# A streaming encoder layer with 32 experts: 16 KB weight rows in 2 MB pieces, and the prompt's output projection inside the sample's attention

## The reference

```python
z = rms(x) @ w_in                          # 1024 x 3080
fox:  8 heads x 64, causal, softmax(q k / 8 + c_q - c_k) v      # c: cumulative log forget
diff: 4 heads, (softmax(q1 k1) - lam * softmax(q2 k2)) v, chunk mask, then rms over 128
h = x + concat(fox, diff) @ w_out
logits = rms(h) @ w_router + b             # 32 experts, top 4, softmax over the 4
y = h + sum over the 4 of gate * (act(rms(h) @ w_gate_up[e] + b) @ w_down[e] + b)
act = min(glu, 7) * sigmoid(1.702 glu) * (clip(lin, -7, 7) + 1)
```

## Time and profile before

| | |
|---|---|
| median of 3 runs | 1375.59 us (1375.3 to 1377.74) |
| profiled execution | 1374.94 us, span 1373.0 us |
| TensorE (PE) busy | 1286.1 us, 94% |
| VectorE (DVE), ScalarE (ACT), GpSimd (POOL) busy | 368.3, 207.2, 145.0 us |
| first pair of experts starts | 418.93 us |
| moved by DMA | 447.1 MB, mean 326 GB/s |

### The profile page before, as it was taken

How to read it: one execution, slowest core, us unless ns; L and a number is a source line. 1 busy time by engine, 2 the same in 40 slices (tenths; PEclk the granted TensorE clock), 3 DMA queues, 4 the chain that set the end, 5 groups by cost and what they waited for, 6 DMA issues and landing times.

```text
span 1373.0 us, 16981 instructions
## 1 busy us (share of the span) xinstructions
PE 1286.1 (94%) x6083; PEld 564.9 (41%) x6084; DVE 368.3 (27%) x959; ACT 207.2 (15%) x524; POOL 145.0 (11%) x340
## 2 busy tenths in 40 slices
PE   6799999999989999999999999999899999999987
PEld 3344445555454443434434344343434434343422
DVE  4223233557251321212212131121213112121311
ACT  5011322255140110101101010010101001010100
POOL 0022300000002101101011010101101010110000
PEclk9999955589989999999999999999999999999997
DMA  8801540046536999999999999999999999999994
GB/s 286 314 32 69 186 152 1 1 153 212 189 136 261 422 413 420 417 416 420 414 422 414 420 416 417 419 414 422 416 419 417 417 420 414 422 413 420 416 417 175
DMA packets 98284, 447.10 MB, mean 326 GB/s; under 512 B 13729, under 2 KB 14002, under 8 KB 65474
## 3 DMA queue, kind: packets, MB, share of 16 engines
q1 hardware_dynamic: 98242, 446.55, 80.8%
HBM read 441.66 MB, written 4.86 MB: 325 GB/s over the span
## 4 chain that ended last, share of the span: by engine, by line
PE 58%; DMA 19%; SPq 17%; DVE 2%; issue 2%; POOL 1%; ACT 1%; DVEq 0%; POOLq 0%; ACTq 0%
DMA arena<-in_w_gate_up 18%; PE psum L1536 15%; SPq L496 13%; PE psum L1568 10%; PE psum L1519 6%; PE psum L1285 5%; PE psum L1433 3%; PE psum L1581 3%; PE psum L1389 3%; PE psum L1341 2%; SPq L386 2%; PE psum L1369 1%; PE psum L1321 1%; PE psum L1557 1%; PE psum L1400 1%
## 5 line engine op out<-in xcount | busy, mean ns | idle before, releaser
L1536 PE MATMUL psum<-arena 128*64 128x512 f32 x2048 | 449.4, 594 | 26.9 <-DMA arena<-in_w_gate_up 26.4
L1536 PEld LDWEIGHTS psum<-arena 128*64 128x64 f32 x2048 | 151.0, 137 | 323.3 <-issue 323.3
L1568 PE MATMUL psum<-arena 128*64 128x512 f32 x1024 | 225.4, 598 | 0.0
L1193 DVE TENSOR_SCALAR arena<-psum 128x256 f32<-128x256 f32 x64 | 27.0, 422 | 439.4 <-PE psum L1536 437.5
L1568 PEld LDWEIGHTS psum<-arena 128*64 128x64 f32 x1024 | 72.5, 138 | 151.7 <-issue 151.7
L1285 PE MATMUL psum<-arena 128*128 128x512 f32 x288 | 127.8, 600 | 0.0
L826 ACT ACTIVATE arena<-arena 128x256 f32<-128x256 f32 x64 | 26.7, 417 | 595.1 <-DVE arena L1193 595.1
L1581 PE MATMUL psum<-arena 128*128 128x512 f32 x192 | 92.5, 616 | 13.1 <-ACT arena L834 13.1
L1519 PEld LDWEIGHTS psum<-arena 128*128 128x128 f32 x768 | 88.5, 194 | 16.1 <-issue 16.1
L1519 PE MATMUL psum<-arena 128*128 128x128 f32 x768 | 91.5, 279 | 3.8 <-POOL arena L593 3.8
L586 POOL COPY arena<-arena 128x6 f32 (+1 forms) x16 | 3.0, 188 | 784.9 <-PE psum L1568 712.9
(11 more groups left out here) (216 smaller groups left out, 893.8 us busy)
## 6 DMA issues: line engine op xcount, KB each, us to landing
arena<-in_w_gate_up SPq DMA_DIRECT2D x256, 1024.0 KB, 22.5
arena<-in_w_down SPq DMA_DIRECT2D x128, 1024.0 KB, 18.5
arena<-in_w_in SPq DMA_DIRECT2D x6, 2048.0 KB, 19.8
arena<-in_cache_fox_k SPq DMA_DIRECT2D x8, 512.0 KB, 3.6
arena<-in_cache_diff_k SPq DMA_DIRECT2D x8, 512.0 KB, 4.4
arena<-in_cache_fox_v SPq DMA_DIRECT2D x8, 512.0 KB, 4.1
arena<-in_cache_diff_v SPq DMA_DIRECT2D x8, 512.0 KB, 5.7
arena<-in_w_out SPq DMA_DIRECT2D x4, 1024.0 KB, 7.6
```

The source lines that it names most:

```text
L1536: last = mm(banks[n][half], XT[u][:, k, half], slot(s[x])[:, 512 * n:512 * (n + 1)], start=False, stop=(k == 7), skip_group_check=True)
L1568: last = mm(banks[hf][half], actT[:, 2 * i + c, half], w, start=False, stop=(i == 3 and c == 1), skip_group_check=True)
```

## The change

- Weights: 12 pieces of 2 MB for each pair through 8 slots. Partition p now holds rows 8p to 8p + 7 of an expert's matrix, so a piece is 16 KB in one run of each partition: two rows of w_gate_up, or four of w_down. From one partition to the next the source steps 64 KB in w_gate_up and 32 KB in w_down. `piece_done` counts after every second k.
- What is multiplied has to follow that order: `scale` writes x2n with its columns regrouped, the activations' products are written with a step of 128 elements, the gains come from a second load (gcol_x) in that order. The transposes of the activations wait for all four quarters.
- The output projection of the prompt's two tiles (n = 0 to 3) is cut into eight halves, one in each of the last eight steps of the sample's attention, all in bank 7, each half in two parts around `turn_probs`. The first half of n waits for `residual(n - 1)`. All mixes now go to bank 6, and mix e waits for the copy of mix e - 1. `turn_out` moves ahead of `turn_probs`.
- The last steps are put in another order: projections 4 and 5 are split around the transposes and the logits, squares 0 and 1 come ahead of the sample's diff norm on ScalarE, routing of tile 1 ahead of the copy of tile 2 on VectorE, gate 0 behind the table. The loads of x_prompt into y are issued earlier, behind `d_done`.

```diff
-PIECES = 24
-RING = 16
-PIECE_W = 2048
-LEAD = 4
+PIECES = 12
+RING = 8
+SLOT_W = 2048
+PIECE_W = 4096
+LEAD = 2
+EARLY = 4
...
+        def out_bank(n):
+            return banks[7] if n < EARLY else banks[n]
+
+        def early_out(i):
+
+            j = i - s_unit[0] - 8
+            return (j // 2, j % 2) if 0 <= j < 2 * EARLY else None
...
-            if r < 16:
-                k = r // 2
-                return io["w_gate_up"][0, bass.ds(e, 1), k * P:(k + 1) * P, :].rearrange("a p n -> p (a n)")
-            k = 2 * ((r - 16) // 2)
-            return io["w_down"][0, bass.ds(e, 1), k * P:(k + 2) * P, :].rearrange("a (c p) n -> p (a c) n", p=P)
+            name, i = ("w_gate_up", r // 2) if r < 8 else ("w_down", (r - 8) // 2)
+            rows_ = io[name][0, bass.ds(e, 1)].rearrange("a (p q) n -> p (a q n)", p=P)
+            return rows_[:, PIECE_W * i:PIECE_W * (i + 1)]
...
+            sp.dma_start(gcol_x, io["ffn_norm"][0].rearrange("(p k) -> p k", p=P)).then_inc(s_gx, 16)
...
+                if b == 6:
+                    sp.wait_ge(scored, s_unit[0])
+                    sp.wait_ge(d_done, DIFF_H)
+                    for t in range(2):
+                        sp.dma_start(y[:, t], io["x_prompt"][0, P * t:P * (t + 1), :]).then_inc(s_xr, 16)
...
-                nc.scalar.activation(x2n[:, t], y[:, t], ACT.Copy, scale=stat[:, 24 + t:25 + t]).then_inc(h_n, 1)
+                nc.scalar.activation(x2n[:, t].rearrange("s (k p) -> s p k", k=8), y[:, t].rearrange("s (p k) -> s p k", k=8),
+                                     ACT.Copy, scale=stat[:, 24 + t:25 + t]).then_inc(h_n, 1)
...
             square(0)
+            square(1)
+            ac.wait_ge(d_ms, DIFF_H + 1)
+            nc.scalar.activation(dsq_s, dsq_s, ACT.Sqrt).then_inc(d_rt, 1)
             root(0)
+            root(1)
             hT_evac(0)
+            hT_evac(1)
             scale(0)
-            square(1)
-            root(1)
+            square(2)
+            root(2)
+            hT_evac(2)
+            scale(1)
+            scale(2)
             gates(0)
...
                     maxes(i + 2)
+                if early_out(i - 1) and early_out(i - 1)[1] == 1:
+                    residual(early_out(i - 1)[0])
                 if 0 <= i + 1 < NA:
                     norms(i + 1)
...
-            residual(2)
-            mean(0)
+            invert(0)
+            invert(1)
             hT_evac(0)
-            residual(3)
-            invert(0)
-            mean(1)
             route(0)
-            gate(0)
             residual(4)
             hT_evac(1)
-            invert(1)
             residual(5)
-            hT_evac(2)
             mean(2)
             route(1)
+            hT_evac(2)
             invert(2)
             route(2)
...
-                    nc.vector.tensor_tensor(act[:, 256 * n:256 * (n + 1)], ta[n % 2], sg[n % 2], ALU.mult
+                    nc.vector.tensor_tensor(act_rows[:, 32 * n:32 * (n + 1)],
+                                            ta[n % 2].rearrange("s (p q) -> s p q", q=8),
+                                            sg[n % 2].rearrange("s (p q) -> s p q", q=8), ALU.mult
                                             ).then_inc(act_ready, 1)
...
-                if e >= 2:
-                    pe.wait_ge(mix_copied, e - 1)
-                O, pt, g = banks[6 + e % 2], pT[e % 2], x["g"]
+                if e >= 1:
+                    pe.wait_ge(mix_copied, e)
+                O, pt, g = mixed_at(e), pT[e % 2], x["g"]
...
+                if 0 <= i - 2 < NA and att[i - 2]["where"] == "s":
+                    turn_out(i - 2)
+                if early_out(i):
+                    n, part = early_out(i)
+                    project_out(n, range(4 * part, 4 * part + 2))
                 if 0 <= i < NA and att[i]["turn"]:
                     turn_probs(i)
+                if early_out(i):
+                    project_out(n, range(4 * part + 2, 4 * part + 4))
                 if 0 <= i - 1 < NA and att[i - 1]["turn"]:
                     mix(i - 1)
-                if 0 <= i - 2 < NA and att[i - 2]["where"] == "s":
-                    turn_out(i - 2)
...
-            project_out(2)
+            pe.wait_ge(mix_copied, NT)
+            project_out(4, range(2))
             pe.wait_ge(d_sq, DIFF_H + 1)
-            pe.wait_ge(mix_copied, NT)
             mm(banks[3], C["ones"], dsq_s, start=True, stop=True).then_inc(d_sum, 1)
             turn_rows(0)
-            project_out(3)
+            project_out(4, range(2, 4))
+            project_out(5, range(4))
+            turn_rows(1)
             logits(0)
             pe.wait_ge(d_done, DIFF_H + 1)
-            project_out(4)
-            turn_rows(1)
-            project_out(5)
+            project_out(4, range(4, 8))
+            project_out(5, range(4, 8))
             logits(1)
...
                 pe.wait_ge(y_added, at_(6, Y_BASE))
+                pe.wait_ge(act_ready, at_(4, 4))
                 for c in range(8):
-                    if c % 2 == 0:
-                        pe.wait_ge(act_ready, at_(4, c // 2 + 1))
```

More of the change, by code:

```diff
@@ L121, in build @@
         gcol = at(take(20), 20)
+        gcol_x = at(take(8), 8)
         lf0 = cur
@@ L159, in build @@
         junk = at(t0, 1024)
-        xs = [at(14 * PIECE_W + 1024 * t, 1024) for t in range(4)]
-        cache = [at((12 + 2 * i) * PIECE_W, 4096).rearrange("p (s t n) -> p s t n", s=4, t=2) for i in range(2)]
+        xs = [at(14 * SLOT_W + 1024 * t, 1024) for t in range(4)]
+        cache = [at((12 + 2 * i) * SLOT_W, 4096).rearrange("p (s t n) -> p s t n", s=4, t=2) for i in range(2)]
         ffv, ffl, nc_p = at(t0 + 2560, NTOK), at(t0 + 1024, NTOK), at(nc0, NKEY_P)
@@ L486, in _ @@
                 sp.dma_start(bdn2[E * hf:E * (hf + 1)], io["b_down"][0, :, 512 * hf:512 * (hf + 1)]).then_inc(s_bdn, 16)
-            for n_ in range(12, 16):
-                sp.dma_start(slot(n_ + LEAD - RING), piece_src(0, n_)).then_inc(ring_in[n_ + LEAD - RING], 16)
+            for n_ in (6, 7):
+                sp.dma_start(piece_slot(n_ + LEAD - RING), piece_src(0, n_)).then_inc(ring_in[n_ + LEAD - RING], 16)
             def refill(it, j):
@@ L1148, in _ @@
                                          AX.X, ALU.max))
+            gate(0)
             gate(1)
@@ L1425, in cum_cached, with project_out @@
                 last.then_inc(cum_done, 1)
-            def project_out(n):
+            def project_out(n, ks):
                 t, hf = n // 2, n % 2
-                if n >= 2:
-                    pe.wait_ge(y_added, n - 1)
-                for k in range(8):
+                if n == 0 and ks[0] == 0:
+                    pe.wait_ge(s_wout, 64)
+                    pe.wait_ge(d_done, DIFF_H)
+                elif n < EARLY and ks[0] == 0:
+                    pe.wait_ge(y_added, n)
+                for k in ks:
                     wv = slot(k // 2).rearrange("p (k n) -> p k n", k=2)
-                    last = mm(banks[4 + n % 2], oT[:, k, P * t:P * (t + 1)], wv[:, k % 2, 512 * hf:512 * hf + 512],
+                    last = mm(out_bank(n), oT[:, k, P * t:P * (t + 1)], wv[:, k % 2, 512 * hf:512 * hf + 512],
                               start=(k == 0), stop=(k == 7))
-                last.then_inc(o_done, 1)
+                if ks[-1] == 7:
+                    last.then_inc(o_done, 1)
             for i in range(-3, NA + 2):
@@ L1531, in pair @@
                 for k in range(8):
-                    s = [arrived(2 * k + x) for x in range(2)]
+                    if k % 2 == 0:
+                        s = [arrived(k + x) for x in range(2)]
                     for n in range(4):
@@ L1535, in pair @@
                             half = slice(SLOTS * x, SLOTS * (x + 1))
-                            last = mm(banks[n][half], XT[u][:, k, half], slot(s[x])[:, 512 * n:512 * (n + 1)],
+                            c0 = 2 * FF * (k % 2) + 512 * n
+                            last = mm(banks[n][half], XT[u][:, k, half], piece_slot(s[x])[:, c0:c0 + 512],
                                       start=False, stop=(k == 7), skip_group_check=True)
-                            if n == 3:
+                            if n == 3 and k % 2 == 1:
                                 last.then_inc(piece_done, 1)
@@ L1566, in pair @@
                                 half = slice(SLOTS * x, SLOTS * (x + 1))
-                                w = slot(s[x])[:, D * c + 512 * hf:D * c + 512 * (hf + 1)]
-                                last = mm(banks[hf][half], actT[:, 2 * i + c, half], w, start=False,
-                                          stop=(i == 3 and c == 1), skip_group_check=True)
-                                if c == 1 and hf == 1:
+                                w = piece_slot(s[x])[:, D * c + 512 * hf:D * c + 512 * (hf + 1)]
+                                last = mm(banks[hf][half], actT[:, 4 * i + c, half], w, start=False,
+                                          stop=(i == 1 and c == 3), skip_group_check=True)
```

(1 more changed line is left out.)

97 lines of the change are left out of this document (46 added, 51 removed).

## The result

| | before | after |
|---|---|---|
| median, us | 1375.28 (1370.98 to 1377.74, 6 runs) | 1381.44 (1379.82 to 1383.89, 6 runs) |
| ratio | | 1.0049, 95% interval 1.0032 to 1.0066 |
| profiled execution, span | 1373.0 | 1379.8 |
| first pair's gate-up starts | 418.93 | 440.40 |
| its last gate-up matmul ends (last pair) | 1334.1 | 1339.9 |

The account below looks back on a forecast made before the run. The prediction took the experts' weight stream as the bound, with the front adding one for one. Stage -16.4, front +17.7 and last pair +0.5 gave +1.8 on 1374.94: about 1376.5 us, own range 1371 to 1382.

Parts of the forecast that it names:

- Rate: Experts' weight stream: 16 KB runs reach 430 GB/s instead of 423 and 410, a gain of 23.3 us.
- Rival 3: Weight stream gains nothing over 8 KB runs: 423 GB/s, 1390 us, chance 0.14; or 387 GB/s, 1473 us, 0.03.
- 2 MB pieces give 3.5 us back at both ends: Experts' stream starts 3.5 us later, and two k instead of one follow the last piece, 3.5 us more.
- Strided products cost nothing: Activation products on VectorE, written with a step of 512 bytes, stay at 0.43 us each.
- Rival 4: Strided products make VectorE the bound of a pair, from 1.1 us each; at 1.74 us each, 1423 us; chance 0.05.
- Last pair +0.5: In the last expert pair, which has no gather, the transposes' wait for all four products shows: +0.5 us.
- Mixes +6.8: Six steps of the sample's attention: with one bank, mixes wait for the copy of the turned output, +6.8 us.
- Adding +3.9: First halves of projections 1, 2, 3 wait for the previous one's residual on VectorE: 1.3 us three times.
- Tile 1's transposes +2.5: Behind attention, tile 1's transposes wait for tile 0's copies, with too little TensorE work to cover: +2.5 us.
- Clock +1.7: Small work ahead of 6.9 us of projection after attention lowers TensorE's clock: 0 to 3.4 us, half taken.
- Rival 1: The front's waits shrink where VectorE or ScalarE gain by the same delay: half the cost, 1367.5 us; chance 0.20.
- Rival 5: Clock falls in the sample's attention's six steps with new waits, doubling 4.3 us of TensorE each: +26, 1402 us; 0.07.

Follow-up runs that it names:

- the run with the old layout: Front and contiguous products of the kernel before, with 2 MB pieces made of whole row blocks (8 and 4 KB runs): 1382.24 us, ratio 1.0057 against before.
- the weight part alone: Kernel before with only the 2 MB pieces, their layout, strided scale and products, and the second gain load: 1360.91 us, ratio 0.9906 against before.
- the front alone: Kernel before, its weights kept, with only the moved projections, one bank for mixes and new order behind attention: 1392.81 us, ratio 1.0124 against before.

## Why the prediction was right, and where not

The forecast was 1376.5 with a range of its own from 1371 to 1382; 1381.4 is at its upper end. Its structure holds: two parts that add, one of -16 on the stream, one of +18 in the front. The two profiles are 6.8 us apart where +1.8 was forecast; of the 5 us between, 4 lie in the front, and the clock is the term that was too small. (The sum on record, 1374.94 + 1.8, is 1376.7, and 1377.4 from the median; it was written as 1376.5.)

- **Rate.** 430 forecast, 428.5 measured. The line through the earlier trace rows was right, its slight overshoot costs 2.5 us over the stream. Rival 3 (423 or less) is out, and the run with the old layout shows that the size of a piece is not the cause.
- **2 MB pieces give 3.5 us back at both ends.** 7.25 - 3.8 = 3.4 at the start, 7.09 - 3.65 = 3.4 at the end. Stage -15.7, forecast -16.4. A pair 58.73, forecast 58.6.
- **Strided products cost nothing.** Wrong in size, right in effect. They take 0.61 us instead of 0.43, hidden in 15 pairs. Rival 4 decides from 1.1 us, so its price was off and its place right. The Trainium skill's rule on new 16-byte lines (SBUF — State Buffer, Door 1) is borne out as to its sign: 0.43 to 0.61 us on VectorE, 1.15 to 2.05 us for the scale on ScalarE, 192 to 335 ns for a weight load. It gives no size, so rival 4 did not follow from it. As the prediction itself says, no row had a write with such a step; that all other rows agree was no evidence.
- **Last pair +0.5.** It was +2.15. The run with 2 MB pieces and contiguous products has 7.56 us there for the 6.84 of before, so waiting for all four products costs 0.7; the step 0.44 (4.48 against 4.04 of wait); the rest, 1.0, is the clock, which was down when the transposes came. The down product was 1.15 shorter, again by the clock; in the weight part alone it took 16.09 us, as before the change.
- **Mixes +6.8.** The six steps grew by 8.5 us, some 6.5 by waits and 2 by clock; undoing it brought the first pair 8.1 us forward. The first four steps grew by 0.95, 0.4, 1.05 and 1.2, as read.
- **Adding +3.9.** Forecast as three times 1.3. The waits were 1.13, 1.14 and 0.27; undoing the first two gave 2.8. In the last steps nothing stands ahead of the turned output, and TensorE already waits there for the copy of the mix. That is 0.42 us three times that I did not name, and it takes the place of the gaps which I let the projections fill (-1.2).
- **End of attention +1.6.** The last mixes stand bare, with gaps of 0.68, 0.41 and 0.32 us, where 0.91 was.
- **Tile 1's transposes +2.5, tile 2's copies +2.0.** 1.99 in this profile, 1.12 in four others with the same order; and 2.95 - 1.27 = 1.7.
- **The gain's load +0.4.** It can't be seen: from kernel to kernel the sample's attention began anywhere between 292.8 and 295.9 us.
- **Clock +1.7.** This is the term that failed. The projection of 6.9 us took 9.02 (+2.1), tile 0's logits 3.32 for 1.87 (+1.4), the first gather 8.32 for 7.17 (+1.2), the attention +2: 6.7 in all. I had split the clock in two, a term for one place and a rival of 26 us for another. What happened lies between: with the new waits the clock fell in the sample's attention in three profiles of three, without them in none of nine, and each such place cost 1 to 3.5 us. Not all of it is due to waits: the first gather took 8.05 us with the front of before too, in the run with the old layout. The mean clock of whole runs says the same: 0.940 to 0.942 in the change, 0.947 to 0.951 before.
- **Sum of the front** 17.7 forecast, 21.5 in the profile (22.6 counted from the start of the six steps, which came 1.2 us earlier by chance), 17 by the ratio of the front alone.

Rival 1 (half the front's cost) did not come: no wait shrank by others' delay except the third adding and tile 1's transposes. Rival 5 came in small: the clock fell in the six steps, for some 2 us instead of 26. That the time still lies in the range is in part luck, since the clock's 5 us too many stood against a range of 5.5 to that side.

## What to carry to other kernels

When a stream of weights bounds a kernel, ask first how long its contiguous runs are and only then how large its transfers are: the rate went 387, 410, 423, 428.5 GB/s with 2, 4, 8, 16 KB and did not move between pieces of 1 and 2 MB, while the larger pieces cost a first slot and a last piece. Work moved into steps in which the engine is busy anyhow gains nothing, and costs what its buffers take from others: here the new front cost 17 us, more than the 13 that the weights gained, and keeping two PSUM banks for the mixes six steps longer returned 8. New waits ahead of TensorE are to be priced with the clock as well: here some 16 us of them went with 6.7 us of halved clock.

## What was not expected of the hardware

- The side on which a step stands matters more than its width. Written with a step of 512 bytes, 256 elements per partition cost VectorE 0.18 us more; read with a step of 32 bytes as weights, 128 columns cost TensorE 143 ns more per load, 6.1 us per gather. In the transposes the same read costs no time that shows (a load takes 190 ns instead of 142, the eight transposes 1.04 us in both).
- The clock falls in different places in profiles of the same instructions: once in the sample's attention of the whole change, twice in that of the front alone. Four runs of one kernel lay 9 us apart along with their mean clock. A gain of 2 or 3 us can only be judged step by step, with the clock of its windows beside it.
